# Seven steps of the widest expert set between the steps of the four smallest, and down weights loaded as pairs of rows

## What is computed

```python
def swiglu(h, w_gu, w_down):
    gu = h @ w_gu
    return (jax.nn.silu(gu[..., :FF_DIM]) * gu[..., FF_DIM:]) @ w_down

def moe_swiglu(h, w_router, w_gu, w_down):
    logits = (h @ w_router).astype(jnp.float32)
    top_vals, top_idx = lax.top_k(logits, TOP_K)
    gates = jax.nn.softmax(top_vals, axis=-1)
    comb = jnp.sum(jax.nn.one_hot(top_idx, N_EXPERTS, dtype=jnp.float32) * gates[..., None],
                   axis=-2).astype(h.dtype)
    y = jnp.zeros_like(h)
    for e in range(N_EXPERTS):
        y = y + comb[..., e:e + 1] * swiglu(h, w_gu[e], w_down[e])
    return y
```

## Time and profile before

| | before |
|---|---|
| median of 3 runs | 1688.39 us (1687.82 to 1688.59) |
| profiled execution | 1692.88 us |
| its span | 1691.1 us |
| TensorE, VectorE, ScalarE busy | 93%, 73%, 61% |
| mean granted TensorE clock | 0.975 of 2.4 GHz |
| read from HBM | 447.63 MB, 265 GB/s over the span |
| loads of the experts | 224 gate and up blocks, 112 down blocks, 1024 KB each |

### The profile page before, as it was taken

The page is one execution under the profiler, slowest core; times in us unless marked ns, Lnnn a source line. Parts: engine busy times, 40 slices in busy tenths (PEclk is TensorE's granted clock), DMA queues, the critical chain, the costliest instruction groups (busy, mean ns, idle before and its releaser), DMA issues.

```text
span 1691.1 us, 22334 instructions
## 1 busy us (share of the span) xinstructions
PE 1580.5 (93%) x7519; PEld 1306.2 (77%) x7520; DVE 1236.1 (73%) x1035; ACT 1038.7 (61%) x924; POOL 125.8 (7%) x83
## 2 busy tenths in 40 slices
PE   8999989999899878899899999999999998988986
PEld 6887878888798767677688888888888776777774
DVE  6745554444489759999998888855555699898995
ACT  4344344434357438888877777744444688888884
POOL 0000000000000004013030030020000120300000
PEclk9999999999999859999999999999999999999997
DMA  9653545555550309999999989956666599999993
GB/s 348 219 194 105 180 145 198 191 182 186 173 173 17 120 27 344 393 385 391 397 377 377 372 309 373 378 177 222 207 203 212 176 387 397 375 393 395 384 394 151
DMA packets 195693, 449.13 MB, mean 266 GB/s; under 512 B 8621, under 2 KB 17357, under 8 KB 195662
## 3 DMA queue, kind: packets, MB, share of 16 engines
q1 hardware_dynamic: 193324, 444.84, 73.4%
q10 hardware_dynamic: 2338, 3.87, 0.6%
HBM read 447.63 MB, written 1.05 MB: 265 GB/s over the span
## 4 chain that ended last, share of the span: by engine, by line
PE 74%; DVE 11%; DMA 7%; issue 5%; ACT 3%; DVEq 0%; POOL 0%; ACTq 0%; POOLq 0%; SPq 0%
PE bank L1271 15%; PE bank L1264 12%; PE bank L1265 11%; DMA raw<-in_moe_w_gu 7%; PE bank L1353 6%; DVE wlo L759 4%; PE bank L1342 4%; PE bank L1262 4%; DVE y L1002 4%; PE bank L1294 2%; PE bank L1301 2%; PE bank L1295 2%; PE bank L1506 2%; PE bank L1344 2%; PE bank L1345 2%
## 5 line engine op out<-in xcount | busy, mean ns | idle before, releaser
L759 DVE TENSOR_TENSOR wlo<-raw,whi 128x2048 fp32r<-128x2048 f32 x422 | 959.8, 2290 | 284.1 <-ACT whi L421 282.4
L421 ACT ACTIVATE whi<-raw 128x2048 fp32r<-128x2048 f32 x422 | 805.5, 1916 | 410.3 <-PE bank L1271 268.8
L1271 PE MATMUL bank<-wlo,xx 128*128 128x512 f32 x1424 | 390.0, 396 | 2.8 <-DVE wlo L759 2.8
L1264 PE MATMUL bank<-whi,xx 128*128 128x512 f32 x848 | 335.9, 396 | 5.7 <-ACT whi L421 2.3
L1265 PE MATMUL bank<-whi,xx 128*128 128x512 f32 x848 | 333.1, 393 | 0.0
L1271 PEld LDWEIGHTS bank<-wlo,xx 128*128 128x128 f32 x1424 | 268.8, 190 | 69.8 <-DVE wlo L759 13.1
L1262 PE MATMUL bank<-whi,xx 128*128 128x512 f32 x576 | 165.2, 409 | 50.2 <-DVE hT L1211 32.6
L1264 PEld LDWEIGHTS bank<-whi,xx 128*128 128x128 f32 x848 | 160.7, 190 | 41.0 <-issue 3.4
L1265 PEld LDWEIGHTS bank<-whi,xx 128*128 128x128 f32 x848 | 160.9, 190 | 32.9
L385 POOL TENSOR_SCALAR onehot<-mats,slot 128x64 fp32r<-128x64 f32 x56 | 114.6, 2069 | 764.6 <-PE bank L1675 764.6
L1262 PEld LDWEIGHTS bank<-whi,xx 128*128 128x128 f32 x576 | 106.3, 193 | 82.9 <-issue 63.1
(11 more groups left out here) (220 smaller groups left out, 1480.5 us busy)
## 6 DMA issues: line engine op xcount, KB each, us to landing
raw<-in_moe_w_gu SPq DMA_DIRECT2D x224, 1024.0 KB, 7.9
raw<-in_moe_w_down SPq DMA_DIRECT2D x112, 1024.0 KB, 8.1
raw<-in_ffn_w_gu SPq DMA_DIRECT2D x28, 1024.0 KB, 5.1
raw<-in_ret_w_in SPq DMA_DIRECT2D x24, 1024.0 KB, 7.6
raw<-in_ffn_w_down SPq DMA_DIRECT2D x14, 1024.0 KB, 4.8
raw<-in_ret_w_out SPq DMA_DIRECT2D x8, 1024.0 KB, 4.9
raw<-in_conv_w_pw SPq DMA_DIRECT2D x16, 512.0 KB, 4.5
raw<-in_conv_w_pw SPq DMA_DIRECT2D x4, 1024.0 KB, 5.0
```

What stands on the lines that cost most here:

```text
L421: nc.scalar.activation(whi[base % SPLIT][:, :], raw[base % RAW][:, :], ACT.Copy).then_inc(hi_done, 1)
L759: nc.vector.tensor_tensor(wlo[base % SPLIT][:, :], raw[base % RAW][:, :], whi[base % SPLIT][:, :].bitcast(f32), ALU.subtract).then_inc(lo_ ...
L1264: nc.tensor.matmul(dst[:, :], xh[:, kc, t, :], wh, start=kc == 0, stop=False)
L1271: last = nc.tensor.matmul(dst[:, :], both, wl, start=False, stop=closing and kc == DC - 1)
```

## The change

The experts are ordered by their token counts at run time. Expert 0 stays first, then come the second and third widest of the other seven, alone as now (`solo`, here experts 3 and 2). The widest of them (expert 4, `SIDE`) has no stage of its own: its seven steps stand between the 28 steps of the four smallest (`MAINS`, here experts 1, 7, 5, 6), two in each round of seven main steps and one in the last. For it there are tiles of their own (`xb0`, `xb1`, `side_onehot`, `side_onehotT`, `acc`); its first tile of tokens keeps its down sums in banks 6 and 7, the second has banks 1 and 3 only for one step and is summed into `acc` by VectorE (`side_sum`) after every wide step. The turned gate and up parts of narrow steps move to banks 0 and 2. Down weights are read as two adjacent rows per partition, 8 KB in one piece instead of two of 4 KB, and the turns therefore read every second column of `hid` and `sgate`.

```diff
+SOLO, MAINS, SIDE = 3, 4, 7
+B_MAIN = B_MOE + SOLO * MOE_BLOCKS
+S_MAIN = STEPS + SOLO * STEPS
+ROUND = STEPS + 2
...
+            def pairs(w, row):
+                return w[bass.ds(row, 256), :].rearrange("(p c) n -> p c n", c=2)
+
             def down(w, base, s, six=0):
                 for r in range(2):
-                    load(base + r, rows(w, s * BANK + r * 256), six)
+                    load(base + r, pairs(w, s * BANK + r * 256), six)
...
+            def solo(x, e):
+                wg, wd = expert(moe_w_gu, x), expert(moe_w_down, x)
                 gu(wg, B_MOE, 0, STEPS * e)
                 with sp.Fori(0, STEPS - 1) as i:
                     gu(wg, B_MOE + 4, i + 1, STEPS * e + i)
                     down(wd, B_MOE + 8, i, STEPS * e + i)
                 down(wd, B_MOE + 40, STEPS - 1, STEPS * e)
+
+            def expert_at(place):
+                return sp.value_load(plan[0:1, 2, bass.ds(place, 1)], min_val=0, max_val=NE - 1)
+
+            solo(0, 0)
+            sp.wait_ge(order_done, 1)
+            with sp.Fori(1, SOLO) as e:
+                solo(expert_at(e), e)
+
+            side_x = expert_at(SIDE)
+            side_g, side_d = expert(moe_w_gu, side_x), expert(moe_w_down, side_x)
+
+            def main_round(i, wg, wd):
+                six = ROUND * i
+                with sp.Fori(0, 2) as j:
+                    gu(wg, B_MAIN + 4, j + 1, six + j)
+                    down(wd, B_MAIN + 8, j, six + j)
+                gu(side_g, B_MAIN + 16, 2 * i, six)
+                down(wd, B_MAIN + 20, 2, six)
+                gu(wg, B_MAIN + 22, 3, six)
+                down(side_d, B_MAIN + 26, 2 * i, six)
+                with sp.Fori(0, 3) as j:
+                    gu(wg, B_MAIN + 28, j + 4, six + j)
+                    down(wd, B_MAIN + 32, j + 3, six + j)
...
+            with sp.Fori(0, MAINS - 1) as i:
+                main_x = expert_at(i + SOLO)
+                main_d = expert(moe_w_down, main_x)
+                main_round(i, expert(moe_w_gu, main_x), main_d)
+                gu(side_g, B_MAIN + 46, 2 * i + 1, ROUND * i)
+                down(main_d, B_MAIN + 50, STEPS - 1, ROUND * i)
+                next_x = expert_at(i + SOLO + 1)
+                gu(expert(moe_w_gu, next_x), B_MAIN + 52, 0, ROUND * i)
+                down(side_d, B_MAIN + 56, 2 * i + 1, ROUND * i)
...
+            def side_y_hi():
+                act.wait_ge(side_done, 1)
+                act.wait_ge(tile1_free, 2 * MAINS)
+                for n in range(2):
+                    nc.scalar.activation(yh[:, 0, n * BANK:(n + 1) * BANK], SIDE_DOWN[0][n][:, :], ACT.Copy).then_inc(yh_done, 1)
+                nc.scalar.activation(yh[:, 1, :], acc[:, :], ACT.Copy).then_inc(side_yh_done, 1)
...
+            def side_sum(used, first):
+                dve.wait_ge(pe_done, used)
+                for n in range(2):
+                    cols = slice(n * BANK, (n + 1) * BANK)
+                    if first:
+                        last = nc.vector.tensor_copy(acc[:, cols], SIDE_DOWN[1][n][:, :])
+                    else:
+                        last = nc.vector.tensor_tensor(acc[:, cols], SIDE_DOWN[1][n][:, :], acc[:, cols], ALU.add)
+                last.then_inc(tile1_free, 1)
+
+            def side_y_lo():
+                for n in range(2):
+                    dve.wait_ge(yh_done, 2 * SIDE + n + 1)
+                    cols = slice(n * BANK, (n + 1) * BANK)
+                    nc.vector.tensor_tensor(yl[:, 0, cols], SIDE_DOWN[0][n][:, :], yh[:, 0, cols].bitcast(f32),
+                                            ALU.subtract).then_inc(yl_done, 1)
+                dve.wait_ge(side_yh_done, 1)
+                nc.vector.tensor_tensor(yl[:, 1, :], acc[:, :], yh[:, 1, :].bitcast(f32), ALU.subtract).then_inc(side_yl_done, 1)
...
+                step_of(B_MAIN + 22, s + 4, WIDE, kind, six)
+                with dve.If(i < 1):
+                    side_sum(B_MAIN + 28 + 6 * six, True)
+                with dve.Else():
+                    side_sum(B_MAIN + 28 + 6 * six, False)
+                with dve.If(i > MAINS - 2):
+                    side_y_lo()
+                with dve.Fori(0, 3) as j:
+                    step_of(B_MAIN + 28, s + 5 + j, kind, kind, six + j)
+                with dve.If(i < MAINS - 1):
...
+                with dve.If(i < MAINS - 1):
+                    for b in range(49, 52):
+                        lo(B_MAIN + b, six)
+                    hidden(s + 8, B_MAIN + 50 + 6 * six, 2)
+                    xl_gathered(i + SOLO + 1)
+                    lo(B_MAIN + 52, six)
+                    lo(B_MAIN + 53, six)
+                    y_lo(i + SOLO + 1)
+                    hTl_evac(s + 9, 2)
+                    lo(B_MAIN + 54, six)
+                    lo(B_MAIN + 55, six)
+                    accumulate(i + SOLO + 1, SCAT_MAIN)
+                    lo(B_MAIN + 56, six)
+                    lo(B_MAIN + 57, six)
+                    with dve.If(need_of(dve, i + SOLO + 1) < 1):
+                        begin(B_MAIN + 52, s + 9, FEW, six)
+                    with dve.Else():
+                        begin(B_MAIN + 52, s + 9, FULL, six)
+                    lo(B_MAIN + 59, six)
+                    side_sum(B_MAIN + 58 + 6 * six, False)
...
             def few_turn(dst, src, how):
                 for c in range(4):
-                    last = nc.tensor.matmul(dst[:, c * HALF:(c + 1) * HALF], src[:, c * P:(c + 1) * P], how[:, 0:HALF],
+                    first = c // 2 * 256 + c % 2
+                    last = nc.tensor.matmul(dst[:, c * HALF:(c + 1) * HALF], src[:, first:first + 255:2], how[:, 0:HALF],
...
+            def main_step(base, s, need, six):
+                pe.wait_ge(silu_done, 2 * s)
+                main_gates(base, need, six)
+                pe.wait_ge(hTl_done, s)
+                main_ups(base, s, need, six)
+                main_rows(base + 4, 0, False, need, six)
+                main_rows(base + 5, 2, False, need, six)
+                main_turn(s, need)
...
+            need = need_of(pe, SOLO)
+            pe.wait_ge(xel_done, SOLO + 1)
+            main_gates(B_MAIN, need, 0)
+            scatter_before(SOLO)
+            pe.wait_ge(hTl_done, S_MAIN)
+            main_ups(B_MAIN, S_MAIN, need, 0)
+            pe.wait_ge(res_done, 2 * SOLO + 8)
+            onehot_turn(1, bank[5]).then_inc(ohT_ps, 1)
+            pe.wait_ge(side_onehot_done, 1)
+            onehot_turn(2, bank[4], side_onehot).then_inc(side_ohT_ps, 1)
+            gather(0, SIDE_DOWN[0], side_onehot)
+            gather(1, SIDE_DOWN[1], side_onehot).then_inc(side_gather_ps, 1)
+            main_turn(S_MAIN, need)
+            pe.wait_ge(ohT_done, SOLO + 1)
+            pe.wait_ge(side_ohT_done, 1)
+            clear(DOWN[0])
+            side_need = need_of(pe, SIDE)
+            with pe.Fori(0, MAINS) as i:
+                six, s = ROUND * i, S_MAIN + ROUND * i
+                need = need_of(pe, i + SOLO)
+                with pe.Fori(0, 2) as j:
+                    main_step(B_MAIN + 4, s + 1 + j, need, six + j)
+                side_products(B_MAIN + 16, s + 3, side_need, six, 2 * i + 1)
+                main_rows(B_MAIN + 20, 0, False, need, six)
+                main_rows(B_MAIN + 21, 2, False, need, six)
+                side_turn(s + 3, side_need)
+                pe.wait_ge(silu_done, 2 * (s + 4))
+                main_gates(B_MAIN + 22, need, six)
+                pe.wait_ge(hTl_done, s + 4)
+                main_ups(B_MAIN + 22, s + 4, need, six)
+                with pe.If(i < 1):
+                    pe.wait_ge(side_xl_done, 1)
+                    clear(SIDE_DOWN[0])
+                side_rows(B_MAIN + 26, side_need, six)
+                with pe.If(i > MAINS - 2):
+                    nothing(bank[6])
+                    nothing(bank[7]).then_inc(side_done, 1)
+                main_turn(s + 4, need)
+                with pe.Fori(0, 3) as j:
+                    main_step(B_MAIN + 28, s + 5 + j, need, six + j)
+                with pe.If(i < MAINS - 1):
+                    side_products(B_MAIN + 46, s + 8, side_need, six, 2 * i + 2)
+                    pe.wait_ge(silu_done, 2 * (s + 9))
+                    pe.wait_ge(onehot_done, i + SOLO + 2)
+                    gather(0).then_inc(gather_ps, 1)
+                    main_rows(B_MAIN + 50, 0, False, need, six)
+                    main_rows(B_MAIN + 51, 2, True, need, six)
+                    side_turn(s + 8, side_need)
+                    pe.wait_ge(xel_done, i + SOLO + 2)
+                    next_need = need_of(pe, i + SOLO + 1)
+                    main_gates(B_MAIN + 52, next_need, six)
+                    pe.wait_ge(hTl_done, s + 9)
+                    scatter(i + SOLO + 1, 1, SCAT_MAIN)
+                    main_ups(B_MAIN + 52, s + 9, next_need, six)
+                    pe.wait_ge(res_done, 2 * (i + SOLO + 1) + 8)
+                    onehot_turn(1, bank[4]).then_inc(ohT_ps, 1)
```

(26 more changed lines are left out.)

432 lines of the change are left out of this document (359 added, 73 removed).

## The result

The changed kernel takes **1702.52 us** (median of 4 runs, 1700.94 to 1703.60), the kernel before 1688.49 us beside it (4 runs): the ratio is 1.0077, with a 95% interval of 1.0063 to 1.0091. So the change costs 0.8%, or 14 us. Its profiled execution is the shortest of its runs, at 1700.94 us with a span of 1699.1 us; between the two profiled spans the difference is 8.0 us.

A forecast was written before the change was run, and what follows sets the result against it. Loads bound narrow experts and TensorE the others; moved under wide steps, narrow steps would be bound by VectorE's chain. Terms summed to 1695.3 against 1691.1 us, 4.2 more, so 1692.6 us, range 1675 to 1711.

The forecast's parts named there:

- code loading: Rival, chance 0.15: TensorE's round loop of some 2,230 instructions doesn't stay resident, four rounds pay 18 us, 1711 us.
- Forecast: Main case, chance 0.50: the chain binds narrow steps, exposed borders and sums eat the gain; own range 1685 to 1701.
- the walk: The whole span as one sum of terms in the new program's order: 1695.3 us against 1691.1.
- the step with `side_y`: Narrow step after the last wide step: the second tile's last sum is followed by `side_y_hi` and `side_y_lo`, 3.7 us more.
- 3 pairs at the expert border: Wide step and the narrow one behind it where the expert changes, with gather, scatter and clear: 52.9 us each, 158.7 together.
- The narrow step: Plain narrow step, bound by the chain from turn through VectorE's splits and `hidT_lo` to the ups: 14.76 us, from 16.0.
- The wide pairs: Wide step and the narrow one behind it, four times within an expert: 44.1 us each, 176.4 together.
- The stride: Turns reading `hid` with a stride of two: taken as 0, up to 52 us if slow; slow-turn rival's chance 0.05.
- The clock: TensorE's clock falls behind nine waits (seven sums, the head, `side_y_hi`): 1.4 us each, 12.6 together.
- signs of being wrong: Narrow steps below 14.5 us, turns over 1, pairs over 48, or instruction packets recurring each round with idle time beside them.
- The waits are cheap: Rival, chance 0.25: the clock doesn't fall in the waits and hand-offs cost nothing, 12.6 + 2 less, 1678.0 us.
- the 345 GB/s: Sign expected in the profile after: load rate through the mixed part, some 345 GB/s with a DMA share below 1.

The follow-up runs named there:

- small loop: Changed kernel with TensorE's code for unused widths taken out of the round loop, 1,244 instructions instead of 2,231: 1686.61 us, ratio 0.9977.
- the kernel with two loops: Changed kernel with two round loops on TensorE, chosen once by the small experts' needs, the one run having 1,462 instructions: 1686.88 us, ratio 0.9986.
- the padded loop of 2,228: The small loop with 984 never executed instructions put back in six places of TensorE's round loop: 1710.23 us, ratio 1.0133.
- that of 1,748: The small loop with 504 never executed instructions put back in the same six places: 1696.01 us, ratio 1.0034.
- 1,993: Changed kernel with only the code for need 3 of the widest expert taken out of TensorE's round loop: 1704.41 us, ratio 1.0092.
- experiment 1: The small loop: changed kernel without TensorE's code for unused widths in the round loop, 1686.61 us, ratio 0.9977 to the kernel before.

## Why the prediction was right in sign and small in size

The forecast was +4.2 us, and the runs have +14.0. The measured time lies in the range only because that was drawn to take in most of the code loading; it is outside the forecast's own range of 1685 to 1701. Forecast and code loading were put as rivals, each to happen without the other. They happen together. In the terms of the walk, from the trace of the changed kernel and of the one with the small loop, which is the forecast's case without code loading (us):

| Term | predicted | changed kernel | small loop |
|---|---|---|---|
| up to the second expert's turn, experts 3 and 2 | 1002.8 | 1000.6 | 1001.4 |
| head with its narrow step and fall | 27.7 | 27.2 | 27.5 |
| 12 plain narrow steps | 177.1 | 178.1 | 176.7 |
| 3 first steps of a round, sum and fall in them | 52.5 | 63.3 | 52.5 |
| 3 steps behind a wide pair, sum and fall in them | 52.5 | 49.8 | 47.8 |
| the step with `side_y` | 23.1 | 21.9 | 21.9 |
| 4 pairs, with the 2.0 for hand-offs | 178.4 | 179.4 | 179.3 |
| 3 pairs at the expert border | 158.7 | 156.1 | 156.1 |
| tail from the last turn | 22.5 | 22.8 | 21.2 |
| sum | 1695.3 | 1699.1 | 1684.4 |

The predicted step with `side_y` is 14.76 + 1.35 + 3.7 + 0.5 and two falls of 1.4.

*The narrow step*, 14.76 us by the chain of the earlier trace rows, was right: 14.83 to 14.86, and 14.76 with unstrided turns. *The wide pairs*, forecast at 44.1, measured 44.70 to 45.14; those at the border 52.03 where I had 52.9. *The stride* I had at nothing by the row nearest to it. It costs 0.04 us a turn, or 5%. The Trainium skill ("SBUF — State Buffer", Door 1), whose rule has no cost here, is off by that much and right against the doubled turn of my upper bound.

*The clock* was mis-sized in number. I took a fall behind each of nine waits. Six came: behind the head (3.6 us of idle time), the three jumps, `side_y` (6.79) and one of the three waits of 2.75 to 2.84 us behind a pair. In the small loop all three waits of 2.33 us at a round's start end in a fall (1.78 to 2.07 us for four products), while none of the three of 2.6 us behind a pair does. Nor does the same place: of the three waits of 2.6 us behind a pair one ends in a fall in the kernel with two loops, two in the padded loop of 2,228 and all three in that of 1,748. So the length of the wait alone doesn't tell, and what does stays open.

*Code loading* is the step that failed: I gave it 0.15, and it is the whole of the loss. My price for it, 4 x 2 x 2.3 = 18 us, was near the 14.7 us between the two spans. The count was wrong twice over: three jumps back, not four rounds, but 5.6 us in each and not 4.6, and with 1.7 us in the tail and a fall of the clock beside. The 2.3 us for a transfer was also a lucky choice: it is that of the router's weights at 467 us, outside the window that the earlier trace rows names, and the other transfer of 32 KB in the kernel before took 4.0 us. Of the signs of being wrong that the prediction gives, the last one came: packets in each round with idle time beside them. I had the numbers for a higher chance, 2,231 instructions against 1,291. The rule of the Trainium skill ("Runtime: NRT & Kernel Launch", Instruction fetch mechanics), by which TensorE holds 2,048 instructions, says that this loop doesn't fit, and the trace agrees. The traces put the point lower, and they decide: at 1,748 there are 2 packets a round and at 1,993 there are 10, though both are under 2,048.

*The rest of the walk* was 10.9 us too long, by the last column. Most of it is 4.7 in the steps behind a wide pair (the falls that didn't come), 2.6 at the borders, 1.4 up to the rounds, 1.3 in the tail, 1.2 in `side_y`. "The waits are cheap", at 1678.0, was thus half right. Without code loading the change would be 0.2% faster than the kernel before (experiment 1), so my sum had the wrong sign for that case, and that the sign came out right was luck: what made the kernel slower was the rival. Among the signs, the 345 GB/s don't follow from the numbers beside them (35 steps of six blocks in 668 us are 330), and the first three rounds had 312 to 318.

## What to carry to other kernels

Count the instructions of a loop before it is made longer, unexecuted branches with the rest: on TensorE loops of up to 1,462 cost nothing here, and with 1,748 and more each round paid. A page of the profile shows it as instruction packets that recur, and as idle time with "issue" behind it at the jump back. Where several widths are possible, choose the loop once outside instead of the width in every helper. And where an engine waits in a chain, ask which result the next instruction really reads: moving one wait behind the up columns was worth 20 us here, more than the whole change cost.

## What the runs showed of the hardware that I had not expected

- Code that is only jumped over costs: 984 unused instructions in six places made the small loop 24 us slower, with 2.67 to 2.97 us of idle time within a group of eight turn products behind a jump, beside 3.87 to 4.12 us at the round's start.
- It isn't all or nothing. With 1,748 instructions a round, 2 packets come and the time lies between (9.4 us over the small loop; by the traces more than half of it in falls of the clock that weren't traced to the code).
- An idle TensorE stops the loads in turn: 7.8 us of it took the DMA engines from 373 to 235 GB/s over 30 us, so in a stretch bound by loads the wait was paid too.
- Branches of a taken path cost little: without those on widths a narrow step is 0.1 us shorter.
